# Two transformer blocks on one core: meta rows scaled by GpSimd and transposed, six fewer products of ones, one inverse root for two norms at the join, one convolution moved into the attention

## The reference

```python
h = concatenate([meta_tokens, x])                      # 272 rows
hn = rms_norm(h, attn_norm)                            # the start
proj = hn @ w_in                                       # then latent, differential and windowed attention
h = h + concatenate([y_a, y_b, y_c]) @ w_out
h = h + (silu(hn @ w_gate) * (hn @ w_up)) @ w_down
x = rms_norm(h, final_norm)[16:]                       # the residual of block two

h = rmsnorm(x, norm_mix)                               # the join
dn_qkv, dn_z, ..., ns_q, ns_ks, ... = split(h @ w_in_2)
q, k, v = split(silu(causal_depthwise_conv(dn_qkv, conv_w)))   # four taps, for the delta rule
ks, kw = rmsnorm(ns_ks, kn_slc), rmsnorm(ns_kw, kn_win)        # keys of the second attention, 64 wide
o_ns = nsa_mixer(...)                                  # compressed, selected and window attention
o_dn = gated_deltanet(q, k, v, ...)
x = x + (sigmoid(gate_dn) * (o_dn @ w_dn) + sigmoid(gate_nsa) * (o_ns @ w_nsa)) @ w_out
x = x + square(relu(rmsnorm(x) @ w_up)) @ w_down
```

## Time and profile before

| | |
|---|---|
| median of three executions | 957.08 us |
| lowest, highest | 955.95, 958.02 us |
| the profiled execution, its own time | 955.19 us |
| its span in the profile | 953.4 us (1.8 us less than its time) |
| TensorE's granted clock, mean over the span | 0.99 of full |

### The profile page before, as it was taken

One profiled execution on the slowest core, in us unless ns is written; L12 is line 12 of the kernel. 1 busy time (PEld: TensorE's weight loads), 2 busy tenths in 40 slices (PEclk: granted clock), 3 DMA queues, 4 the chain that ended last, 5 costly groups with the idle time before them and its releaser, 6 DMA issues. The chain is left out here.

```text
span 953.4 us, 17694 instructions
## 1 busy us (share of the span) xinstructions
PE 922.3 (97%) x6958; PEld 828.8 (87%) x6958; DVE 636.9 (67%) x1338; ACT 466.9 (49%) x925; POOL 156.2 (16%) x111
## 2 busy tenths in 40 slices
PE   9999899999999999997799999999999999999998
PEld 8897688999999989886688888998888899999996
DVE  4657766666556687798997977545966665455543
ACT  6554655545344562753334674354453464454441
POOL 1100000000000015006565315000000022233221
PEclk9999999999999999999799999999999999999999
DMA  6830334556556445646232101022546546555651
GB/s 242 260 128 1 116 128 122 182 183 223 160 191 216 144 140 180 223 157 216 74 127 87 48 14 67 3 69 90 177 175 202 183 147 221 178 177 177 195 182 44
DMA packets 38578, 139.31 MB, mean 146 GB/s; under 512 B 4325, under 2 KB 4581, under 8 KB 38496
## 3 DMA queue, kind: packets, MB, share of 16 engines
q1 hardware_dynamic: 37152, 134.10, 42.9%
q10 hardware_dynamic: 816, 2.25, 0.7%
q0 software_dynamic: 528, 1.84, 0.7%
HBM read 137.09 MB, written 1.08 MB: 145 GB/s over the span
## 5 line engine op out<-in xcount | busy, mean ns | idle before, releaser
L1835 DVE TENSOR_TENSOR parts<-raw,parts 128x1024 fp32r<-128x1024 f32 (+2 forms) x225 | 286.6, 1310 | 131.7 <-ACT parts L1322 127.0
L1322 ACT ACTIVATE parts<-raw 128x1024 fp32r<-128x1024 f32 (+2 forms) x225 | 228.1, 1050 | 115.8 <-PE psum L532 96.3
L530 PE MATMUL psum<-hT,parts 128*128 128x256 f32 (+1 forms) x928 | 264.6, 285 | 14.4 <-DVE scr L2236 13.2
L531 PE MATMUL psum<-hT,parts 128*128 128x256 f32 (+1 forms) x928 | 263.4, 284 | 0.0
L532 PE MATMUL psum<-hT,parts 128*128 128x256 f32 (+1 forms) x928 | 261.6, 282 | 0.0
L530 PEld LDWEIGHTS psum<-hT,parts 128*128 128x128 f32 x928 | 175.5, 189 | 17.9 <-DVE scr L2236 13.4
L532 PEld LDWEIGHTS psum<-hT,parts 128*128 128x128 f32 x928 | 176.9, 191 | 0.0
L531 PEld LDWEIGHTS psum<-hT,parts 128*128 128x128 f32 x928 | 175.9, 190 | 0.6
L530 PE MATMUL psum<-parts,arena_r 128*128 128x512 f32 x344 | 135.1, 393 | 0.9 <-DVE arena_r L1850 0.7
L532 PE MATMUL psum<-parts,arena_r 128*128 128x512 f32 x344 | 134.0, 389 | 0.0
L531 PE MATMUL psum<-parts,arena_r 128*128 128x512 f32 x344 | 133.9, 389 | 0.0
(11 more groups left out here) (328 smaller groups left out, 1211.4 us busy)
## 6 DMA issues: line engine op xcount, KB each, us to landing
raw<-weights SPq DMA_DIRECT2D x247, 512.0 KB, 4.1
raw<-weights SPq DMA_DIRECT2D x4, 384.0 KB, 4.7
X<-x SPq DMA_DIRECT2D x2, 512.0 KB, 5.1
out<-X SPq DMA_DIRECT2D x2, 512.0 KB, 2.6
arena<-lines POOLq DMA_DIRECT2D x1, 768.0 KB, 9.6
cbuf<-consts ACTq DMA_DIRECT2D x1, 561.0 KB, 6.4
arena<-lines POOLq DMA_DIRECT2D x1, 544.0 KB, 7.8
arena<-params ACTq DMA_DIRECT2D x1, 512.0 KB, 5.5
```

The lines of the kernel that those rows point to most:

```text
L530: mm(ps, a, c, start=start, stop=False)
L531: mm(ps, a, d, start=False, stop=False)
L1322: signal(A(split_slot(name)[0], whole_piece, ACT.Copy), "first_parts")
L1835: signal(V_.tensor_tensor(second, whole_piece, first.bitcast(F32), ALU.subtract), "split_vector")
```

## The change

At the start: `turner_meta` goes. POOL multiplies the 16 meta rows by their inverse roots, as soon as `rms1` is there, into `Xnm` (sem `meta_norm`), and PE transposes them against the identity (one pass in place of two). PE makes 40 products of ones in place of 46.

At the join: the final norm's variance is kept in columns 62 and 63 of `st`, beside the 16 sums of the key norm, and one `inv_sqrt` of 18 columns serves both. The `inv_sqrt` of 2 columns and the call that split the six pieces ahead of it go; X is scaled right behind k's third half, and the six pieces are split behind that, when `convolve` of k's fourth half asks for its job. The first half of v is made at group 0 of the attention, as the first of two fillers there (on PE and DVE alike). ACT splits what it had split for silu of k's fourth half, but applies that silu behind the attention.

```diff
-        FILL = [0, 1, 3, 4, 7, 10, 13]
+        FILL = [0, 0, 1, 3, 4, 7, 10, 13]
...
-            busy(10)
+            busy(4)
...
-            pe.wait_ge(sem("norm1"), 2)
+            pe.wait_ge(sem("norm1"), 1)
+            pe.wait_ge(sem("meta_norm"), 1)
...
-                mm(ps[:, 0:META], one["Xm"][0:META, cols], turner_meta, start=True, stop=True)
+                nc.tensor.transpose(ps[:, 0:META], one["Xnm"][0:META, cols], ident[0:META, 0:META])
...
-            for what in EARLY:
-                conv_half(*what)
...
-            for half in range(4):
+            for half in range(3):
                 silu_conv(0, 4 * (half // 2), half % 2)
+            conv_pieces(0, 4, 1)
...
             attention(G2, extra)
-
+            silu_conv(0, 4, 1)
...
+            pool.wait_ge(sem("rms1"), 1)
+            nc.gpsimd.tensor_scalar(one["Xnm"][0:META, :], one["Xm"][0:META, :], st[0:META, 6:7], None, ALU.mult)\
+                .then_inc(sem("meta_norm"), 1)
...
-            signal(V_.tensor_scalar(turner_meta, ident[0:META, 0:META], st[0:META, 6:7], None, ALU.mult), "norm1")
...
-            inv_rms(st[:, 80:96], st[:, 64:80], ND, st[:, 128:144], st[:, 160:176])
+            link(V_.tensor_scalar(st[:, 64:80], st[:, 64:80], 1.0 / ND, EPS, ALU.mult, ALU.add))
+            inv_sqrt(st[:, 36:54], st[:, 62:80], st[:, 128:146], st[:, 160:178])
...
-            second_parts(beyond("cv_k3"))
-            inv_sqrt(st[:, 4:6], st[:, 30:32], st[:, 0:2], st[:, 24:26])
...
-            for what in EARLY:
-                convolve(*what)
```

More of the change, by code:

```diff
@@ L1109, in _ @@
             pairs = [(t, q) for t in range(TT) for q in range(2)]
-            extra = {i: [lambda w=what: conv_half(*w)] for i, what in zip(FILL, FILLERS)}
+            extra = {}
+            for i, what in zip(FILL, CONVOLVED):
+                extra.setdefault(i, []).append(lambda w=what: conv_half(*w))
             extra |= {i: [lambda w=what: decay_rows(*w)] for i, what in zip(DECAYS, pairs)}
@@ L1654, in _ @@
                         release(ins, name)
-            for what in EARLY + FILLERS:
+            for what in CONVOLVED:
                 silu_conv(*what[1:])
@@ L2354, in _ @@
             pairs = [(t, q) for t in range(TT) for q in range(2)]
-            extra = {i: [lambda w=what: convolve(*w)] for i, what in zip(FILL, FILLERS)}
+            extra = {}
+            for i, what in zip(FILL, CONVOLVED):
+                extra.setdefault(i, []).append(lambda w=what: convolve(*w))
             extra |= {i: [lambda w=what: decay_rows(*w)] for i, what in zip(DECAYS, pairs)}
```

13 lines of the change are left out of this document (6 added, 7 removed).

## The result

The changed kernel takes 949.82 us (median of 6 runs, 949.01 to 951.63); the kernel before took 957.38 beside it (6 runs, 955.95 to 958.37). The ratio is 0.9926, 95% interval 0.9912 to 0.9939. So it is faster, as forecast, but by 7.6 us and not by 14.3, and 949.8 lies outside the range of 940.0 to 947.5. The profiled execution of after is the slowest of its six, 951.63 us, with a span of 949.8.

A forecast was written before the change was run, and what follows sets the result against it. PE, busy 922 of 953 us, was taken as the bound. Join -13.19 - 1.51 + 0.4 = -14.3 us, start 0.2 - 1.0 + 0.8 = 0.0; from the median 957.08 that gives 942.8 us, range 940.0 to 947.5.

The forecast's parts named there:

- (a): Join: the 11 root steps go from between k's third and fourth half; two more columns in the key norm's root cost nothing.
- (b): Join: X scaled at 430.1, not 453.7, for 2.48 us, covered by DVE's idle 3.82 us; PE loses 0.4 us.
- (c): Join: last two splits still start at 438.55; k's fourth half is convolved by 444.6 to 446.8.
- (d): Join, PE: the 13.19 us wait is gone; the clock stays at full, 1.51 us more.
- rival 4: Join: the wait has another cause and PE stands still as long in group 0; 954 to 957 us, chance 0.02.
- What is late next: Attention's first three groups: DVE takes peaks and two halves, stays ahead by 1 to 3 us; the shift is passed on.
- Rival 1: Attention: POOL's splitting holds DVE's negations of peaks in three groups; +2 to +4, 945.5 to 947 us, chance 0.13.
- (f): Start: six products of ones fewer are 12 passes, 1.34 us, so PE is free at 12.2.
- (g): Start: POOL's meta multiplication takes 2.2 us; PE starts at 13.8, not 13.60, +0.2 us (-0.9 to +1.5).
- (h): Start: one pass of four fewer for each of eight blocks, 0.13 us each, -1.0 us.
- (i): Start: the clock may fall sooner, so the transpositions run at half too; +0.8 us (0 to +1.7).
- Rival 2: Start: meta rows come after 15, or the clock comes back later; +2 to +4, 945 to 947 us, chance 0.13.

The follow-up runs named there:

- roots_late: Changed kernel with ten products of ones, the residual's root steps and six splits again between k's third and fourth half, ahead of X's scaling; 955.65 us, ratio 0.9984.
- no_pool_sub: Changed kernel in which POOL leaves out the subtraction for the twelve pieces of dv1, dq0 and dq1; 942.07 us, ratio 0.9856.
- neg_act: Changed kernel with ten products of ones and the negation of the second attention's peaks on ScalarE, not VectorE; 938.79 us, ratio 0.9815.
- ones_kept: Changed kernel with ten products of ones behind the squares in place of four; 946.88 us, ratio 0.9906.
- join_alone: Changed kernel with the start of the kernel before, so the join's edits alone; 947.34 us, ratio 0.991.
- meta_dve: Changed kernel with the meta rows multiplied on VectorE, not POOL, still four products of ones; 945.55 us, ratio 0.9884.

## Why the prediction was wrong, point by point

**(a), (b), (c), (d): right.** The steps are gone, X is scaled in 2.48 us, the four splits take 4.63, k's fourth half is let go at 447.1 (444.6 to 446.8 forecast, and the start 2.6 late), and the wait of 13.19 us is gone, with no standstill and the clock at 1.00 up to 465. `roots_late` shows that these steps made the wait, and rival 4 is out. The sum of -14.3 is about what A to B brings where VectorE isn't late afterwards: `no_pool_sub` has -14.6, `neg_act` -15.0. Such closeness is in part luck, since both also take work from POOL or VectorE that the change left in place.

**"What is late next": the step that failed.** I followed VectorE through the peaks of the first three groups, found it ahead by 1 to 3 us, and passed the whole shift on to the end; what VectorE does behind these groups I put at nothing without a reason. In these groups the lead was there: TensorE's only wait from 440 to 472 is 0.34 us. The standstill comes some groups later, at 481 to 490, where VectorE has a result to finish for each group beside the peaks and a half of q, while POOL still splits what it had split in pauses before. Before, this didn't happen, for two reasons that went with the wait of 13.19 us: TensorE stood still until VectorE had come up to it, and POOL, which waited for TensorE to free its next piece's slot, paused for 11.18 us up to 464.42 and left VectorE undisturbed. Some 7.7 us were given back (`ones_kept` against `neg_act` from A to B; 8.1 in the medians).

**Rival 1** was this mechanism, at +2 to +4 with 0.13. It was mis-sized in three ways: I priced only the negations (the longest steps are the additions at L2331, 2.2 us each), only in the first three groups, and without the clock. The very term I priced didn't grow: the negations of these three groups took 0.37, 1.55 and 0.17 us in after, 2.1 in all, against 2.3 before. (Its own sum gives 944.8 to 946.8, not 945.5 to 947.) The kernel before already had held negations further on, on VectorE's timeline:

```profile
482.70 2.31 DVE L1934 TENSOR_SCALAR npeaks<-peaks 128x4 f32<-128x4 f32 x1
```

I had looked at this stretch as harmless, since TensorE hardly waited there then (0.34 us at 477.54, 1.07 at 496.16).

**The start.** (f) was right: the ones end at 11.93 (12.2 forecast). (g) was mis-sized: 3.42 us for the multiplication, not 2.2; the row with the same operation was the near one, that with the same size was not. TensorE starts at 14.61, not at 13.8. (h) is right at full clock, 0.53 us a block in `ones_kept`, and not seen in after, since the blocks run at half. (i) is what failed: I gave the clock +0.8 (0 to 1.7) for an earlier fall of the same length. It is at half three times as long, 10.2 us and not 3.4. By `ones_kept` all of the start's loss is this: 4.2 us at mark A in the profiled executions, of which that of after is its slowest, and 1.9 to 2.6 over all executions. I had also taken the 3.4 us at half of one trace for a fixed part of the start; `join_alone`, with the same start, has none.

Beside (i) I had weighed a rule of the Trainium skill (TensorE: Matmul & The Clock Gate, Part 4: PE-mode transpose), that transpositions don't count as work for the clock gate. `ones_kept` and `meta_dve` speak against its use here: all eight blocks of transpositions run at 1.00 and the clock stays there to 26 us.

**Rival 2**, with 0.13, was a late start at +2 to +4, by meta rows after 15 or by more time at half clock. The second came true, with 6.8 us more at half where I had 3.4, and the size about (1.5 to 2.6). The first did not: POOL's row starts at 10.93, right when the root is ready, and ends at 14.35, so nothing of a load of code is seen. The Trainium skill (GPSIMD Engine Reference, 2.1 Instruction dispatch) has about 6 us for that, and puts them at the first call of freshly loaded code; that they would end at 9.2 was my reading of it. This call took 3.42 us in all, so no such 6 us are in it. Whether a load passed unseen in the 7.7 us in which POOL waited, or there was none, no run here shows.

**Chances.** Each rival had 0.13 and both together 0.04, and both came, the second by half of its cause. (The chances of the outcomes that are faster add up to 0.96, not 0.95.) They were rated as if VectorE's lead and the clock were safe unless something failed. The profile gave two reasons for doubt: the earlier trace rows had VectorE busy 12.8 of 13.2 us at the very place, and the earlier trace rows had TensorE's ones as the only thing between a standstill and the transpositions.

## What to carry to other kernels

When a long wait goes, list what the other engines did in it: here a pause of POOL and a catching-up of VectorE were lost with it, and the engine that ended the wait is the first candidate for the next bound, some groups later and not at once. An engine that is late by little can be worth all of the loss: 3.6 us taken from VectorE by the additions, or 6.7 by the negations, brought 7 and 8. Filler products ahead of transpositions are not waste where TensorE would stand still otherwise: six of them, 1.3 us, brought 1.9 to 2.6, but eight in the attention brought no gain in the median, because VectorE was late there.

## What the runs showed of the hardware

- Whether POOL holds up a VectorE step goes by the step's operands. With POOL at a subtraction, an addition of SBUF and SBUF took 2.22 us (0.42 free), a negation in SBUF 1.98 (0.17), but a reciprocal from SBUF to SBUF 0.17, and `scalar_tensor_tensor` with one input in PSUM and one in SBUF 0.86 for four. POOL's copies hold too: L2328 took 0.95 us in `neg_act`, beside a copy from 463.09 to 464.13, and 0.23 free.
- POOL's TENSOR_SCALAR with a scalar from a column takes 3.42 us on 16 x 1024, VectorE's 0.73. On 128 x 256 POOL took 0.85, a quarter for a quarter of the columns and eight times the rows: in these two its time went by the columns.
- A VectorE step with both inputs in SBUF, 0.17 us free, took 1.02 at 11.64 beside that multiplication and ended at 12.66, though POOL's row runs to 14.35. A subtraction with both inputs in SBUF took 1.22 at 12.99, as in before (1.23): there, at least, VectorE wasn't held for as long as the row lasts.
- Half clock costs less where TensorE has to wait for another engine anyway: 10.2 us at half, 5.1 us of work, cost 2.2 in the attention, where VectorE was late. At the start the same 10.2 us cost 4.2 (mark A of after against `ones_kept`).
